# Attention without GpSimd: rotary products on VectorE from PSUM, splits on ScalarE and VectorE, x loaded first

## The reference

```python
proj = x @ w_in
A: multi-head latent attention, 4 heads (64 plain + 32 rotary columns), dense over 512 keys
B: sc_b * dwconv3(sc_c * sc_h)
C: silu(layer_norm(dwconv31(a * sigmoid(gate)) + b))
D: windowed attention |i-j| <= 128, 4 query and 2 key heads of 64, rotary, a sink logit per head
x = layer_norm(alpha * x + concat(A, B, C, D) @ w_out)
x = layer_norm(alpha * x + moe(x))     # top-64 tokens per expert, silu(x Wg) * (x Wu) @ Wd
rope(x1, x2) = (x1*cos - x2*sin, x2*cos + x1*sin)
```

## Time and profile before

| | |
|---|---|
| median of 3 runs | 1646.81 us (1643.65 to 1647.55) |
| profiled execution | 1641.34 us, span 1639.5 us, mean granted TensorE clock 0.940 |
| TensorE busy | 1364.5 us (83%) |
| VectorE busy | 499.9 us (30%) |
| ScalarE busy | 291.5 us (18%) |
| GpSimd busy | 238.9 us (15%) |
| chain that ended last | PE 59%, DMA 22%, DVE 9%, issue 5%, POOL 2%, ACT 2% |
| expert weights on SP's queue | 192 pieces, 62.6% of the DMA engines' time |

### The profile page before, as it was taken

One profiled execution on the slowest core, in us unless ns is written; L12 is line 12 of the kernel. 1 busy time (PEld: TensorE's weight loads), 2 busy tenths in 40 slices (PEclk: granted clock), 3 DMA queues, 4 the chain that ended last, 5 costly groups with the idle time before them and its releaser, 6 DMA issues.

```text
span 1639.5 us, 14715 instructions
## 1 busy us (share of the span) xinstructions
PE 1364.5 (83%) x5984; PEld 679.4 (41%) x5984; DVE 499.9 (30%) x871; ACT 291.5 (18%) x503; POOL 238.9 (15%) x170
## 2 busy tenths in 40 slices
PE   3989688759999889889699868883899999889883
PEld 3755446623333333333277444673333333233231
DVE  4754472421111101101459354445011111101105
ACT  2334260200010000000143424301000010000000
POOL 0543250000000000000255234210000000000003
PEclk9999889869999999999999978886899999999997
DMA  9100123579999999999850003216899999999991
GB/s 385 65 1 1 52 78 141 205 276 429 428 427 426 428 427 428 428 427 427 362 193 1 1 1 129 97 60 280 336 428 427 428 427 428 428 426 428 428 426 79
DMA packets 42483, 462.63 MB, mean 282 GB/s; under 512 B 6704, under 2 KB 7344, under 8 KB 14000
## 3 DMA queue, kind: packets, MB, share of 16 engines
q1 hardware_dynamic: 31968, 432.62, 62.6%
q10 hardware_dynamic: 6416, 14.39, 2.5%
q0 software_dynamic: 4032, 14.68, 2.4%
HBM read 451.18 MB, written 10.49 MB: 282 GB/s over the span
## 4 chain that ended last, share of the span: by engine, by line
PE 59%; DMA 22%; DVE 9%; issue 5%; POOL 2%; ACT 2%; ACTq 0%; POOLq 0%; DVEq 0%
DMA ring<-w_moe 18%; PE bank L793 17%; PE bank L477 10%; PE bank L814 10%; PE bank L766 7%; DMA X<-out 2%; PE bank L434 2%; PE bank L622 2%; PE bank L542 1%; PE bank L726 1%; PE bank L730 1%; PE bank L729 1%; DVE ring L1081 1%; DMA X<-x_in 1%; PE bank L575 1%
## 5 line engine op out<-in xcount | busy, mean ns | idle before, releaser
L793 PE MATMUL bank<-ring,work 128*64 128x512 f32 x2048 | 451.9, 598 | 33.9 <-DMA ring<-w_moe 22.1
L793 PEld LDWEIGHTS bank<-ring,work 128*64 128x64 f32 x2048 | 166.3, 138 | 309.5 <-issue 251.7
L814 PE MATMUL bank<-ring,work 128*64 128x512 f32 x1024 | 231.2, 597 | 28.1 <-DMA ring<-w_moe 16.4
L1249 DVE TENSOR_TENSOR X<-X,bank 128x512 f32<-128x512 f32 x128 | 87.8, 686 | 314.2 <-PE bank L766 314.0
L1237 DVE TENSOR_TENSOR work<-work,bank 128x512 f32<-128x512 f32 x32 | 22.0, 688 | 500.9 <-PE bank L793 499.2
L814 PEld LDWEIGHTS bank<-ring,work 128*64 128x64 f32 x1024 | 77.0, 136 | 170.1 <-issue 143.1
L766 PE MATMUL bank<-work 128*128 128x512 f32 x256 | 125.5, 620 | 13.1 <-ACT work L1513 11.2
L1502 ACT ACTIVATE work<-bank 128x512 f32<-128x512 f32 x64 | 38.3, 598 | 358.3 <-PE bank L434 358.3
L1642 POOL COPY cur<-slot_i 128x1 int32<-128x1 int32 x16 | 2.9, 184 | 611.5 <-PE bank L434 554.3
L477 PE MATMUL bank<-x_hi,w_hi 128*128 128x512 f32 x288 | 80.7, 426 | 3.5 <-ACT x_hi L1307 3.5
L1554 POOL TENSOR_SCALAR stat<-stat 128x1 f32<-128x1 f32 x16 | 9.9, 620 | 501.6 <-DVE stat L881 501.3
(11 more groups left out here) (189 smaller groups left out, 1462.5 us busy)
## 6 DMA issues: line engine op xcount, KB each, us to landing
ring<-w_moe SPq DMA_DIRECT2D x192, 2048.0 KB, 29.2
ring<-w_in SPq DMA_DIRECT2D x18, 1024.0 KB, 16.3
ring<-w_out SPq DMA_DIRECT2D x8, 1024.0 KB, 23.0
out<-X POOLq DMA_DIRECT2D x12, 512.0 KB, 9.1
X<-out ACTq DMA_DIRECT2D x2, 2048.0 KB, 16.6
x_rows<-X ACTq DMA_DIRECT2D x8, 512.0 KB, 2.6
X<-x_in ACTq DMA_DIRECT2D x4, 512.0 KB, 12.9
work<-ln SPq DMA_DIRECT2D x2, 1024.0 KB, 9.4
```

The lines of the kernel that those rows point to most:

```text
L793: ins = mm(B((kind, pair, n))[64 * e:64 * e + 64, :], xsT[:, k, 64 * e:64 * e + 64], w[:, e, n * 512:(n + 1) * 512], start=(k == 0), stop= ...
L814: ins = mm(B(("O", pair, n))[64 * e:64 * e + 64, :], hidT[:, k, 64 * e:64 * e + 64], w[:, i, e], start=(k == 0), stop=(k == KD - 1))
L1249: nc.vector.tensor_tensor(X[:, t, cols], X[:, t, cols], B(name)[:, :], ALU.add)\
```

## The change

- SP's queue loads x tile by tile before the weights; each tile has its own semaphore, and TensorE, ScalarE and POOL begin with the first. The angles move on VectorE behind the splits of x and of slot 0, the sines on ScalarE behind the high part of slot 1.
- Rotary: VectorE multiplies a projected block straight from PSUM with the cosines and with the sines (`turned_parts`); TensorE adds both, one times the identity, one times the turning constant, into one bank (`roped`), and ScalarE copies that out. The rotary columns of all four query heads of group A become one block `("qup", 2)` (the host reorders `w_uq`), and the key goes to all heads in one broadcast copy.
- POOL keeps the low parts of slots 1 to 7 and the small LayerNorm operations. VectorE takes slot 8, `wout_lower`, the subtractions `mix_lower` and group B's products (from PSUM); ScalarE takes the high parts `mix_higher`.
- Block 12 is projected before the head loop, the other fifteen passes are spread one to a step; `d_norm(2)` goes ahead of the short convolution. The fetch of x is issued at step 9 of group A.
- Fifteen matmuls whose result nobody reads stand in the routing: ten behind the transposes of the affinities, five behind those of the chosen slots.

```diff
             sp.dma_start(cst[:], consts).then_inc(consts_in, 16)
-            sp.dma_start(slot_iota[:], iota).then_inc(consts_in, 16)
+            for t in TILE_ORDER:
+                sp.dma_start(X[:, t], x_in[t * P:(t + 1) * P]).then_inc(x_in_tile[t], 16)
...
-                def turned_by(name, rows):
+                def roped(name, ready, turn, cosines, sines, rows=slice(0, P)):
+                    pe.wait_ge(rope_parts, at(lay, 5, ready))
                     before(pe, name, lay)
-                    mm(B(name)[:, :], rot_d, rows, start=True, stop=True).then_inc(fullsem(name), 1)
+                    mm(B(name)[rows, :], ident[rows, rows], cosines, start=True, stop=False)
+                    mm(B(name)[rows, :], turn[rows, rows], sines, start=False, stop=True)\
+                        .then_inc(fullsem(name), 1)
...
+                pe.wait_ge(params_in, at(lay, 64, 64))
+                pe.wait_ge(lat_ready, at(lay, 3, 3))
+                for t in range(3):
+                    q_up(t)
+                for j in range(3):
+                    read_out(pe, ("ropeD", j), lay)
+                d_scores(0, 0)
+                d_scores(0, 1)
+                pe.wait_ge(cconv_ready, at(lay, 2, 2))
+                summed(("mean",), (mix[:, YC], mix[:, YC + 1]))
+                roped(("ropeK",), 4, rot_a, a_parts[r, 0], a_parts[r, 1], r)
+                k_up(0)
+                roped(("ropeQ",), 5, rot_a, a_parts[:, 2], a_parts[:, 3])
+                d_scores(0, 2)
+                d_scores(0, 3)
+                project(SC_C, HI_HI, HI_LO, LO_HI)
+                k_up(1)
+                v_up(0)
+                v_up(1)
                 pe.wait_ge(csq_ready, at(lay, 2, 2))
                 summed(("var",), (csq[:, 0], csq[:, 1]))
...
+                def fill(g):
+                    project(SC_C + 1 + g // 3, (HI_HI, HI_LO, LO_HI)[g % 3])
                 for n in range(NT - 1):
-                    first, second = SC_C + 2 * n, SC_C + 2 * n + 1
-                    d_turned(n, 0)
-                    d_scores(n + 1, 0)
-                    project(first, HI_HI)
-                    d_turned(n, 1)
-                    d_scores(n + 1, 1)
-                    project(first, HI_LO)
-                    d_turned(n, 2)
-                    d_scores(n + 1, 2)
-                    project(first, LO_HI)
-                    if n == 0:
-                        read_out(pe, ("gvT",), lay)
-                    d_values(n, 0)
-                    d_turned(n, 3)
-                    d_scores(n + 1, 3)
-                    if n == 0:
-                        q_rotated()
-                    project(second, HI_HI)
-                    project(second, HI_LO)
+                    for h in range(GQ_H):
+                        d_turned(n, h)
+                        d_scores(n + 1, h)
+                        if (n, h) == (2, 3):
+                            for name in (("qup", 0), ("qup", 1), ("kup", 0), ("kup", 1), ("ropeK",), ("ropeQ",)):
+                                read_out(pe, name, lay)
+                            a_scores(0)
+                        else:
+                            fill(6 * n + h)
+                        if h == 2:
+                            if n == 0:
+                                read_out(pe, ("gvT",), lay)
+                            d_values(n, 0)
+                    if n < 2:
+                        fill(6 * n + 4)
+                    else:
+                        a_scores(1)
                     d_values(n, 1)
-                    project(second, LO_HI)
-                pe.wait_ge(keys_ready, at(lay, 1, 1))
-                pe.wait_ge(queries_ready, at(lay, MLA_H, MLA_H))
-                for j in range(MLA_H // 2):
-                    read_out(pe, ("kup", j), lay)
-                a_scores(0)
-                a_scores(1)
+                    if n < 2:
+                        fill(6 * n + 5)
+                    else:
...
+                def unread(times):
+                    for i in range(times):
+                        mm(B(("O", 0, i % 2))[:, :], ident, cos_d[:], start=True, stop=True)
+                unread(10)
...
+                unread(5)
...
+                if lay == 0:
+                    angles()
...
+                def turned_parts(name, ready, cosines, sines, scale, parts, rows=slice(0, P)):
                     full(v, name, lay)
-                    nc.vector.tensor_tensor(tmp_d[:, j], B(name)[:, :], sin_d[:], ALU.mult)\
-                        .then_inc(freesem(name), 1)
+                    src = B(name)[rows, :]
+                    nc.vector.scalar_tensor_tensor(out=parts[0], in0=src, scalar=scale, in1=cosines[rows, :],
+                                                   op0=ALU.mult, op1=ALU.mult).then_inc(parts_begun, 1)
+                    nc.vector.scalar_tensor_tensor(out=parts[1], in0=src, scalar=scale, in1=sines[rows, :],
+                                                   op0=ALU.mult, op1=ALU.mult).then_inc(rope_parts, 1)
...
+                    if tap == 10:
+                        d_parts_of(0)
...
+                    if tap == 21:
+                        d_parts_of(1)
...
+                def gated(j):
...
+                    nc.vector.tensor_tensor(prod[:, j, 1:1 + S], B(("in", SC_H + j))[:, :], scc[:, j], ALU.mult)\
...
+                def out_gated(j):
...
+                    nc.vector.tensor_tensor(mix[:, YB + j], B(("in", SC_B + j))[:, :], scc[:, j], ALU.mult)\
...
+                def w_lower_last():
+                    n = IN_SLOTS - 1
+                    v.wait_ge(w_hi_ready, at(lay, IN_SLOTS, n + 1))
+                    nc.vector.tensor_tensor(w_lo[n], ring[:, n], w_hi[:, n % 2].bitcast(F32), ALU.subtract)\
+                        .then_inc(w_last_ready, 1)
+                def wout_lower(n):
+                    j = MIX_ORDER[2 * n] // 2
+                    v.wait_ge(wout_hi_ready, at(lay, 4, n + 1))
+                    nc.vector.tensor_tensor(wout_low[j], ring[:, OUT_RAW[j]], wout_hi[j].bitcast(F32), ALU.subtract)\
+                        .then_inc(wout_lo_ready, 1)
+                def mix_lower(n):
+                    v.wait_ge(split_hi, at(lay, 6, 2 * n + 2))
+                    for k in MIX_ORDER[2 * n:2 * n + 2]:
+                        nc.vector.tensor_tensor(mix_lo[:, k], mix[:, k], mix_hi[:, k].bitcast(F32), ALU.subtract)\
+                            .then_inc(split_ready, 1)
...
-                hold(rope_d_ready, at(lay, 3, 3))
-                k_sine()
+                turned_parts(("in", KROPE), 4, cos_a, sin_a, 1.0, (a_parts[r, 0], a_parts[r, 1]), r)
+                turned_parts(("qup", 2), 5, cos_a, sin_a, MLA_SCALE, (a_parts[:, 2], a_parts[:, 3]))
                 d_max(0)
                 cf_centred()
-                k_rope()
                 d_norm(0)
                 d_max(1)
-                q_sines()
+                wout_lower(0)
+                d_norm(1)
+                gated(0)
+                w_lower_last()
                 cf_scaled()
-                d_norm(1)
                 d_max(2)
-                q_rope()
+                wout_lower(1)
+                d_norm(2)
+                gated(1)
                 short_conv()
+                out_gated(0)
                 cf_gated()
-                d_norm(2)
                 d_max(3)
+                out_gated(1)
                 a_max(0)
                 a_max(1)
                 d_norm(3)
@@ -1149,6 +1175,10 @@
                     if 3 <= i + 2 < NT * MLA_H:
                         a_max(i + 2)
                     a_norm(i)
+                    if i in (2, 7):
...
+                    if i in (2, 7):
+                        wout_lower(2 + i // 7)
+                    if i in (4, 5, 8):
+                        mix_lower((4, 5, 8).index(i))
...
-            for t in range(NT):
-                ac.dma_start(X[:, t], x_in[t * P:(t + 1) * P]).then_inc(x_in_sem, 16)
...
+                if lay == 0:
+                    ac.wait_ge(angles_ready, 1)
+                    act(sin_d[:], trig[:, 3], ACT.Sin).then_inc(sines_ready, 1)
+                    ac.wait_ge(angles_ready, 2)
+                    act(cos_d[:], trig[:, 4], ACT.Sin).then_inc(sines_ready, 1)
+                    ac.wait_ge(sines_ready, 2)
...
+                copy_out(("ropeK",), Kh[r, :, :],
+                         B(("ropeK",))[r, :].unsqueeze(1).broadcast_to([ROPE, MLA_H, S]))
+                keys_out(0)
+                for h in range(MLA_H):
+                    copy_out(("ropeQ",), Qh[r, h, :], B(("ropeQ",))[ROPE * h:ROPE * (h + 1), :],
+                             frees=(h == MLA_H - 1))
+                d_exp(0)
+                copy_out(("in", SC_C), scc[:, 0])
...
-                    if i in (1, 4):
+                    if i in (0, 4):
                         wout_high(2 + i // 4)
+                    if i == 1:
+                        ac.wait_ge(yc_ready, at(lay, 2, 2))
+                        mix_higher(0)
+                    if i == 2:
```

(8 more changed lines are left out.)

329 lines of the change are left out of this document (115 added, 214 removed).

## The result

The changed kernel takes 1553.83 us (median of four runs, 1552.50 to 1561.09; the kernel before beside it 1647.18), a ratio of 0.9446 with a 95% interval of 0.9414 to 0.9479. The profiled execution took 1553.28 us, its span 1551.3. The prediction was 1574, with a range of 1550 to 1607; it was 20 us too high.

The account below looks back on a forecast made before the run. Weight stream bounds the expert part; in attention TensorE waits for VectorE, VectorE for POOL. Twice 36 a layer plus 7 gave 79 off 1641.34: 1562; median offset 5.5: 1568; less 3 a layer of gain: 1574, range 1550 to 1607.

Parts of the forecast that it names:

- The start: Layer 0, once: first projection 12.4 us earlier through x loaded first, of which 7 us kept, between 3 and 12.
- The step that failed: Long convolution at the start: begins some 3 us behind the projections' shift at worst, VectorE's 3.8 us room absorbs it.
- The step before it: Angles on VectorE, blocked by POOL's split, end near 37.5; so the fifth projection starts at 44.7 instead of 52.94.
- The head loop and the way into A: Attention, up to group A's first transposes: norm first, products on VectorE; 25 us a layer gained, bounds 12 and 28.
- rival one: Inserted work meets TensorE: loop gains 12, group A loses 5, routing 0; 37 us off, 1610; chance 0.22.
- Group A: Group A's stretch of 33.9 us: blocks go, splits, subtractions and copies come in; 1 us longer, from -3 to +5.
- The reload: Fetch of x issued at step 9: TensorE's 6.3 us wait and 3.3 of clock go, 9.5 us a layer.
- Routing: Before the experts: fifteen unread matmuls fill waits and keep the clock up, 2.5 us a layer, or 0.
- The discount of 3 us a layer: Whole layer: 3 us a layer taken off the gain for stands that such a sum overlooks, giving 1574.
- the stream: Rival in the expert part: the weight stream hides the layers' whole gain, 1640 to 1647; chance 0.04.
- the clock: Rival from head loop to group A's end: TensorE sits at 1.2 GHz, at worst 31 us slower, 1678; chance 0.03.

Follow-up runs that it names:

- the yardstick: The changed kernel run once more, unaltered, beside the kernel before: 1550.8 us, ratio 0.9435.
- the convolution on time: Changed kernel with four small loads asked for at ScalarE's start and the long convolution waiting for the parameters alone: 1545.6 us, 0.9408.
- the angles out of the way: Changed kernel with VectorE's angle arithmetic ahead of its splits of x: 1552.22 us, 0.9447.

## Why the prediction was right, and where it was off

**The start: wrong.** Predicted 7 us kept, between 3 and 12; 3.7 were (11.0 earlier, 8.6 given back, of which 1.3 belong to the layer's own new work, as in layer 1). In the yardstick's trace the same marks give 5.9: the same wait (2.12 us there) stands in it, but the pass behind it took 2.39 us, where the first trace had 3.46 at the lower clock level. The cost, then, is 2.5 to 5 us, against 8.5 kept with the convolution on time. The step that failed is "VectorE has 3.8 us of room there before TensorE's query projections end, so nothing is added". The convolution started 5.6 us behind the shift of the projections (9.2 less 3.6), where I had at worst 3. The room is at its end, but the new rotary products stand inside its queue and TensorE wants the first of them at 62. The step before it was right by luck: the fifth projection came at 43.75 (predicted 44.7), and a VectorE angle operation was held up beside POOL (one of the three in the row of 6.43 took 4.99), yet with the angles out of the way it comes at 43.86. TensorE's own twelve passes, which follow each other without a gap from 18.97 and begin at the lower clock level (granted 0.72 to 0.80 between 18 and 30 us), set it.

**The head loop and the way into A: right in mechanism, small in size.** 25 us a layer predicted; 28.0 and 27.0 measured, with the start's loss taken out of layer 0. First transposes to last score took 46.62 in both layers (predicted 48.6), last score to A's transposes 10.55 and 13.80 (11). The spread of the second number is the clock behind the 1.78 us wait. That the four splits on VectorE fit, where rival one had them meet TensorE, is borne out. How the 27 to 28 us divide is shown only for the norm's place (5.4 and 6.6 us when taken back). The larger part, for the rotary and group B's products and the block moved ahead, rests on the waits that are gone between the two traces.

**Group A: the sign was wrong.** Predicted 1 us longer; 2.2 and 6.2 shorter. I set the work coming in (8.8 us on VectorE, 3.5 on ScalarE) against some 4 us of blocks. The run with the splits back on POOL shows the blocks at 5.9 us a layer, and VectorE fits: in the yardstick it is busy for 18.9 of the first 20 us, and TensorE's transposes wait for it 3.3 us in all. In layer 1 the old kernel had lost more, with two blocked operations.

**The reload: right.** 9.5 predicted; 9.0 and 9.2 up to the last router product in the two traces, 8.6 and 8.3 when taken back.

**Routing: right by the run without it** (2.2 us in layer 0 and 2.5 in layer 1), although between the two traces only 0.7 and 2.1 us show in the two layers. The expert part of layer 0 is 1.5 us longer without the unread matmuls (480.8) than in the kernel before (479.2), which has none either; 0.9 of it lies in the first stretch (30.34 against 29.46), and what it is stays open.

**The 20 us.** The terms sum to 88.1 where I had 79: 9 us. Within them the start's loss of 3.3 hides behind gains that were put too low, above all group A's 3 and 7. The discount of 3 us a layer for overlooked stands was not needed: 6. And I added the 5.5 us by which the median shown stood above the profiled execution, as if it belonged to the kernel; after the change that distance is 0.5, and in four later comparisons the kernel before had medians of 1642 to 1645: 5. Of the rivals, neither the stream nor the clock decided anything; first expert matmul to the next layer is 479.2 us in both kernels.

## What to carry to other kernels

Give a load that is awaited first a semaphore of its own; behind one count the smallest early need waits for the last and slowest load. When work moves from one engine to another, look for the consumer inside the queue it joins, not only at the queue's end. A short stand of TensorE can cost more than its length through the clock, and freeing the bank one instruction sooner gives both back.

## What the runs showed of the hardware

- A 64 KB load in 64-byte pieces, the last of four on its queue, took 29.7 us beside a weight stream on another queue; a 48.5 KB one, first in its queue, took 7.9 us. The two queues' packets went one for one (222 and 223 in 4 us), whatever their size.
- With the same instructions and the same 1.78 us wait, TensorE's clock fell to half for 3 to 10 us or did not fall; over eleven executions it fell in 12 of 22 stretches, and one stretch took from 8.07 to 12.76 us by it.
- A VectorE normalization in SBUF that meets a POOL split ends with the split (4.08 and 4.81 us instead of 0.49), and so did a product of the angles (4.99 instead of 0.7); an operation that reads PSUM and one SBUF operand beside such a split is not slowed (0.56).
- POOL's first split stood until its own store of x had landed, though no semaphore asks for that and its operand was ready at 20.7 (15.47 us of idle at 27.93, while the store's last packets moved between 26 and 27; 17.43 before, and 11.42 in layer 1). Why it waits for its own stores was not tried.
